# Two-layer diffusion trunk on one core: earlier modulation products and two weight loads outside the ring in layer 0

## The reference

```python
for l in range(2):
    sh, sc, g, shf, scf, gf = split6(silu(c) @ w_mod[l] + b_mod[l])     # modulation, per group
    h = rmsnorm(x) * (1 + sc) + sh
    if l == 0:
        q, k, v = split(h @ w_in_ab)            # 1024 x 2304; q and k normalised, sample rotated
        o = concat(grouped_query_attention, differential_attention) @ w_out_ab
    else:
        q, k, v = split(h @ w_in_c)             # 1024 x 3072
        o = attention(q, k, v) @ w_out_c
    x = x + g * o
    x = x + gf * moe(rmsnorm(x) * (1 + scf) + shf)   # 16 experts of 3 x 1024 x 1024, top 2
```

## Time and profile before

| what | value |
|---|---|
| median of three runs | 1276.59 us |
| span of the profiled execution | 1273.4 us |
| time of the profiled execution outside its span | not listed; the median is 3.2 us above the span |
| moved by DMA | 494.07 MB, 388 GB/s over the span |
| TensorE busy | 92% |
| VectorE, ScalarE, GpSimd busy | 22%, 15%, 4% |
| granted TensorE clock, mean | 0.978 |

### The profile page before, as it was taken

One profiled execution on the slowest core, in us unless ns is written; L12 is line 12 of the kernel. 1 busy time (PEld: TensorE's weight loads), 2 busy tenths in 40 slices (PEclk: granted clock), 3 DMA queues, 4 the chain that ended last, 5 costly groups with the idle time before them and its releaser, 6 DMA issues.

```text
span 1273.4 us, 13823 instructions
## 1 busy us (share of the span) xinstructions
PE 1174.6 (92%) x5485; PEld 514.1 (40%) x5485; DVE 283.2 (22%) x681; ACT 187.6 (15%) x441; POOL 56.4 (4%) x68
## 2 busy tenths in 40 slices
PE   4999999999888989899989999999998989888998
PEld 2445463343333434243334454643433434343333
DVE  1156441201020210101233443312020110102013
ACT  1234221100000101001022341210000101000010
POOL 0513000000000000000011100000000000000000
PEclk9999999999999999999999999899999999999999
DMA  9959999999999999999993679789999999999996
GB/s 376 340 207 353 419 419 427 428 415 431 426 429 429 428 428 429 429 428 428 416 393 85 262 263 424 305 366 421 376 428 428 428 429 428 429 429 429 428 429 256
DMA packets 58495, 494.07 MB, mean 388 GB/s; under 512 B 5314, under 2 KB 6482, under 8 KB 27732
## 3 DMA queue, kind: packets, MB, share of 16 engines
q1 hardware_dynamic: 55408, 485.85, 91.9%
q0 software_dynamic: 2864, 7.46, 1.8%
q10 hardware_dynamic: 180, 0.17, 0.0%
HBM read 490.69 MB, written 3.16 MB: 388 GB/s over the span
## 4 chain that ended last, share of the span: by engine, by line
PE 65%; DMA 25%; issue 3%; DVE 2%; POOL 2%; ACT 2%; SPq 1%; POOLq 0%; DVEq 0%
PE bank L1050 40%; DMA ring<-in_w_gate 10%; PE bank L825 9%; DMA ring<-in_w_up 9%; PE bank L835 3%; PE bank L1020 3%; PE bank L1011 3%; DMA ring<-in_w_in_ab 2%; PE bank L794 2%; DMA ring<-in_w_down 2%; PE bank L772 2%; DMA ring<-in_w_mod 1%; DMA gbuf<-gate_rows 1%; PE bank L1100 1%; POOL hss L672 1%
## 5 line engine op out<-in xcount | busy, mean ns | idle before, releaser
L1050 PE MATMUL bank<-ring,hT 128*64 128x512 f32 x2816 | 638.9, 609 | 63.8 <-issue 29.2
L1050 PEld LDWEIGHTS bank<-ring,hT 128*64 128x64 f32 x2816 | 213.9, 140 | 464.3 <-issue 462.5
L825 PE MATMUL bank<-ring,hT 128*128 128x512 f32 (+1 forms) x352 | 148.3, 580 | 3.9 <-DMA ring<-in_w_in_ab 2.4
L825 PEld LDWEIGHTS bank<-ring,hT 128*128 128x128 f32 x352 | 66.6, 192 | 79.6 <-issue 76.3
L1803 DVE TENSOR_TENSOR work<-work,bank 128x512 f32<-128x512 f32 x56 | 38.5, 688 | 188.6 <-PE bank L1020 188.4
L1796 DVE TENSOR_TENSOR work<-work,bank 128x512 f32<-128x512 f32 x32 | 22.0, 688 | 238.5 <-PE bank L1050 238.5
L1837 DVE COPY work<-bank 128x512 f32<-128x512 f32 x16 | 11.1, 691 | 228.9 <-PE bank L1050 212.4
L1011 PE MATMUL bank<-work 128*128 128x128 f32 x512 | 60.4, 277 | 0.0
L1011 PEld LDWEIGHTS bank<-work 128*128 128x128 f32 x512 | 59.3, 194 | 0.0
L835 PE MATMUL bank<-ring,work 128*128 128x512 f32 x128 | 56.5, 595 | 0.7 <-DVE work L1624 0.7
L1354 ACT ACTIVATE hT<-bank 128x512 f32<-128x512 f32 x32 | 19.0, 595 | 250.3 <-PE bank L1100 250.3
(11 more groups left out here) (211 smaller groups left out, 668.0 us busy)
## 6 DMA issues: line engine op xcount, KB each, us to landing
ring<-in_w_gate SPq DMA_DIRECT2D x64, 2048.0 KB, 17.2
ring<-in_w_up SPq DMA_DIRECT2D x56, 2048.0 KB, 17.2
ring<-in_w_down SPq DMA_DIRECT2D x56, 2048.0 KB, 16.9
ring<-in_w_mod SPq DMA_DIRECT2D x23, 2048.0 KB, 12.5
work<-in_w_up SPq DMA_DIRECT2D x8, 2048.0 KB, 20.9
ring<-in_w_in_c SPq DMA_DIRECT2D x6, 2048.0 KB, 21.1
ring<-in_w_in_ab SPq DMA_DIRECT2D x4, 2048.0 KB, 21.5
ring<-in_w_down SPq DMA_DIRECT2D x8, 1024.0 KB, 16.8
```

The source lines that it names most:

```text
L825: ins = pe.matmul(b[:, 0:n], hT[:, c, t * P:(t + 1) * P], w[:, c, 0:n], start=c == 0, stop=c == DC - 1)
L1050: ins = pe.matmul(bank[banks[j]][64 * e:64 * e + 64, :], lhs[:, 4 * h + c, 64 * e:64 * e + 64], weights(e, c, j), start=(h, c) == (0, 0), ...
```

## The change

The table `FILL` of layer 0 is written anew. Six modulation units of layer 0 are used between the projections of the prompt ahead of the first turn, and four of those that were used in turns 0 to 3 leave them. Input unit 4 of the prompt is used before its units 1, 2 and 3. Two units are loaded outside the ring: input unit 4 into `gbuf`, and modulation unit (0, 1, 2) into the buffers of the probabilities. ScalarE waits for the use of the latter before the first exponentials. `rot` moves to the buffer of the transposed q and k. The first two expert units of layer 0 are issued ahead of the up units outside the ring (`free = 2`, before 0). Layer 1's table is unchanged.

```diff
 FILL = {
     0: {"front": [("in", 0, 1), ("hT", 0, 0), ("in", 1, 1), ("in", 2, 1), ("in", 3, 1)],
-        "head": [("in", 4, 1), ("in", 0, 0), ("in", 1, 0)],
-        "keys": [("in", 2, 0)],
-        "scores": [("in", 3, 0)],
...
+        "head": [("in", 4, 1), ("mod", 0, 1, 0), ("in", 0, 0), ("mod", 0, 1, 1), ("in", 4, 0)],
+        "keys": [("mod", 0, 1, 2), ("mod", 0, 1, 3), ("in", 1, 0)],
+        "scores": [("mod", 0, 2, 0), ("in", 2, 0), ("mod", 0, 2, 1), ("in", 3, 0)],
...
+APART = {("in", 0, 4): "gbuf", ("mod", 0, 1, 2): "probs"}
+def ring_units(l):
+    return [u for u in dense_units(l) if u not in APART]
...
-        rot = work[:, 11264:13312]
+        rot = work[:, 8192:10240]
+        in_gbuf = gbuf[:, :, :].rearrange("p c n -> p (c n)").rearrange("p (c n) -> p c n", c=DC)
+        in_probs = work[:, 11264:15360].rearrange("p (r n) -> p r n", r=2)
...
-                free = 2 * l
+                free = 2
...
-            for g in range(N0):
+            for u in dense_units(0):
+                if u in APART:
+                    if u[0] == "in":
+                        sp.dma_start(in_gbuf, unit_src(u)).then_inc(gbuf_unit_loaded, 16)
+                    else:
+                        l, group, k = u[1:]
+                        sp.wait_ge(filled, fill(("hT", 0, 0, 0, 1)))
...
+                if (l, j) == (0, 0):
+                    act.wait_ge(mod_used, mods_used["mod", 0, 1, 2])
```

More of the change, by code:

```diff
@@ L107 @@
     0: {"front": [("in", 0, 1), ("hT", 0, 0), ("in", 1, 1), ("in", 2, 1), ("in", 3, 1)],
-        "head": [("in", 4, 1), ("in", 0, 0), ("in", 1, 0)],
-        "keys": [("in", 2, 0)],
-        "scores": [("in", 3, 0)],
[L111 to L115, removed]
+        "head": [("in", 4, 1), ("mod", 0, 1, 0), ("in", 0, 0), ("mod", 0, 1, 1), ("in", 4, 0)],
+        "keys": [("mod", 0, 1, 2), ("mod", 0, 1, 3), ("in", 1, 0)],
+        "scores": [("mod", 0, 2, 0), ("in", 2, 0), ("mod", 0, 2, 1), ("in", 3, 0)],
+        0: [("modT", 1), ("mod", 0, 2, 2)],
+        1: [("T", 0), ("mod", 0, 2, 3)],
+        2: [("mod", 1, 0, 0)],
+        3: [("oT", 1), ("mod", 1, 0, 1)],
+        4: [("wo", 0, 1)],
         5: [("wo", 1, 1)],
-        (6,): [("mod", 1, 0, 0)],
-        6: [("oT", 0)],
-        (7,): [("mod", 1, 0, 1)],
+        (6,): [("modT", 2)],
[1 row of a table added]
         7: [("hT", 1, 1), ("wo", 0, 0), ("rt", 1), ("wo", 1, 0), ("rc",), ("xT",), ("mod", 1, 0, 2),
@@ L368, in build @@
         ld_bias = sem("ld_bias")
+        gbuf_unit_loaded, probs_unit_loaded = sem("gbuf_unit_loaded"), sem("probs_unit_loaded")
         turns = sem("turns")
@@ L423, in build @@
                 k += 1
-        units = dense_units(0) + dense_units(1)
-        N0 = len(dense_units(0))
+        units = ring_units(0) + ring_units(1)
+        N0 = len(ring_units(0))
         mods_used = {u: i + 1 for i, u in enumerate(u for l in range(LAYERS) for u in released(l) if u[0] == "mod")}
         unit_no = {u: i for i, u in enumerate(units)}
-        free_order = [released(l) for l in range(LAYERS)]
+        free_order = [[u for u in released(l) if u not in APART] for l in range(LAYERS)]
         place, MOE_RING = {}, []
@@ L432, in build @@
             first = list(range(SLOTS)) if l == 0 else [MOE_RING[0][(i - OUTSIDE) % SLOTS] for i in range(SLOTS)]
-            mine = dense_units(l)
+            mine = ring_units(l)
             assert sorted(mine) == sorted(free_order[l])
@@ L628, in experts @@
                 return more
-            for g in range(N0):
+            for u in dense_units(0):
[5 more added lines that the diff above has]
+                        sp.wait_ge(filled, fill(("hT", 0, 0, 0, 1)))
+                        src = a["w_mod"][l].rearrange("(p r) n -> p r n", r=8)[:, 2 * k:2 * k + 2, GC * group:GC * (group + 1)]
+                        sp.dma_start(in_probs, src).then_inc(probs_unit_loaded, 16)
+                    continue
+                g = unit_no[u]
                 if g >= SLOTS:
@@ L777, in mod @@
                 halves = (l, group, k) == (0, 0, 3)
-                w = rows2[3 if halves else arrived(("mod", l, group, k))]
+                if ("mod", l, group, k) in APART:
+                    pe.wait_ge(probs_unit_loaded, 16)
+                    w = in_probs
+                else:
+                    w = rows2[3 if halves else arrived(("mod", l, group, k))]
                 if k == 0 and 3 * l + group:
@@ L818, in project @@
             def project(l, u, t):
-                w = ring[arrived(("in", l, u))]
                 n = unit_cols(("in", l, u))
+                if ("in", l, u) in APART:
+                    pe.wait_ge(gbuf_unit_loaded, 16)
+                    w = in_gbuf
+                else:
+                    w = ring[arrived(("in", l, u))]
                 b = bank_free(("qkv", l, u, t))
```

## The result

| kernel | median us | range | runs |
|---|---|---|---|
| before, beside the changed one | 1278.84 | 1272.77 to 1281.72 | 8 |
| changed | 1284.95 | 1284.05 to 1288.06 | 8 |

The ratio is 1.0053, with a 95% interval of 1.0040 to 1.0066: the change makes the kernel slower, by 6.1 us as the difference of the medians and by 6.8 us as the ratio has it. The profiled execution of the changed kernel took 1288.06 us, the slowest of its eight and 3.1 over its median, with a span of 1285.2 us and a mean granted clock of 0.974 (0.978 before). So the two profiles differ by more than the medians do; I compare places in them, not their ends.

A forecast was written before the change was run, and what follows sets the result against it. Layer 0's dense part was taken as TensorE-bound, its expert part as load-bound. From 1276.6, 5.1 us for later pair 2 units plus 1.0 for clock gave 1282.7 us; the range was 1274 to 1288.

The forecast's parts named there:

- The loads: Layer 0's dense part: loads land early, cost TensorE nothing; the 2.1 us wait at 205.04 goes, DMA engines idle there.
- Steps 1 and 2: Prompt's projections, then its q and k norm: projection about 14 us later, norm at 121.7; TensorE waits about 3.1 us.
- Step 3: Ahead of turn 4's scores: `modT` 1 lengthens VectorE's chain; TensorE waits 4.3 to 4.4 us, plus net 0.7 at turn 2's values.
- Step 4: Turns 3 to 5 of the attention: stay covered by one modulation product each and the output projections.
- Step 5: After the sample's second output projection: the chain takes 5.8 us against 2.8 of TensorE work; it waits 3.0 us.
- M: Start of the first expert product: forecast 198.7 us, from 188.5 plus 10.2 of added waits.
- From M to pair 2's last product: Expert part of layer 0: last units land at M + 141.8, from restart, 127.3 us of loads and 5.0 of slot waits.
- The sum: Pair 2's last units land at 340.5 against 335.4, 5.1 us later, and the shift stays; 1 us of clock added.
- the break-even: First expert product at 193.6 us, 5.1 us of added wait, where early loads and added waits cancel.
- That the early loads win: Rival: the chain stays covered, first expert product at 188.5, pair 2's last units at 330.3, kernel 1271.5 us; chance 0.12.
- That the two cancel: Rival: added TensorE waits and early loads balance, 1.4 to 8.9 us of wait, about 1277 to 1279 us; chance 0.22.
- That the loads collide with GpSimd's: Rival: GpSimd's small loads come late during the projections and delay the sample's transposes, some 1285 us; part of chance 0.66.

The follow-up runs named there:

- the order alone: Against the changed kernel: its order of work kept, but all units in the ring and the gate units where they were before; 1289.51 us, ratio 1.0084.
- the four early products: Against the changed kernel: only modulation group 1 used early, the other filler back in the turns; 1279.49 us, ratio 1.0004; run again 1279.7 us, ratio 1.0012.

## Why the prediction was right, by its steps

**The loads.** 60 to 120 us carries 371 to 387 GB/s ("well over 300"), no product waits for a load there, the up units come in time, and the hole near 204 is there. The fourth load of group 1 was to land at 75 us and landed at 79.0 (issued at 66.46, 12.5 us on its way), so it had 4.4 us to spare before its use and not 8. The cost of loads for TensorE was rightly taken at nothing in this order. It would not have been in the others: the order alone pays 3.6 us for late units, and four products in a row pay 4.19.

**Steps 1 and 2.** q and k were to come 14 us later; it was 15.05. A modulation product standing by itself takes 1.86 us from start to start (64.47 to 66.33 in the changed kernel), not the third of three in a row, 1.79, and the sample's transposes at 79.54 waited 0.57 us (0.31 before), which no step had. These two make about half of the 1.05 us. The waits of 1.0 and 2.1 us were 0.87 and 2.02.

**Step 3.** The wait of 4.3 to 4.4 us measures 4.0 at the full clock, and stands in two places. The kernel where `modT` 1 is moved shows its 1.5 us in the chain. The 0.7 us at the values of turn 2 were 0.54, 0.35 net.

**Step 4.** Turns 3 to 5 show no wait above 0.2 us.

**Step 5.** 3.0 us was over-sized: 2.14, in four waits and not one. The cause was named only in part. With `modT` 2 moved away from there the waits still add up to 2.22 us, so VectorE's work for it is not what opens them; what the run leaves is that nothing fills TensorE.

**M.** 198.7 was forecast and 201.04 measured. Of the 2.3 us between them 1.6 is the low clock inside the dense part, which the sum had booked elsewhere as 1 us. The granted clock was 0.50 in two stretches, behind the waits of 2.02 and 2.23 us. The Trainium skill, "TensorE: Matmul & The Clock Gate", section "Part 1: The HAM clock gate", has the clock follow how busy the engine has been; by that rule, which speaks against a change that thins the filler, the prediction would have put the full 1.7 us in place of 1. The trace agrees in the size, with 1.6. It doesn't show that such a wait always costs clock: the same wait of 2.01 us left it at 1.00 in the kernel with `modT` 2 moved.

**From M to pair 2's last product.** 141.8 was forecast; 143.0 was measured, and 142.9 to 143.3 in the eight other profiles in which modulation units were used early. The mis-sized term is the restart: the first two units issued at 208.2, behind the first product, landed at 215.9 and 221.8, so 13.6 us after their issue where the sum had 2.45 + 9.8 = 12.3.

**The sum.** Pair 2's last product was forecast 5.1 us later and stood 8.6 us later in these two profiles. That "the shift stays" from there on is not what these two profiles show: it was 11.9 us at layer 1's first expert product. The medians differ by 6.1 us, the very sum forecast, and by 5.1 to 8.4 within the interval. So the forecast was right in its sign, its mechanism and its size, but that it fits to 0.1 us is luck: M and the restart were 3.5 us short together, of which the 1 us for the clock makes good only a part, and the profiles' later growth has no place in it. The absolute time, 1282.7, lies 2.3 us under the result, as much as the median of before's eight runs lies over that of the three it started from (1278.84 against 1276.59). Two bounds were added up loosely: 12 us of wait and 1.7 of clock give 1285.2 and not 1286, and 3.8 us under the break-even is 1.3 us of wait and not 1.4.

**The rivals.** That the early loads win: the kernels with before's order and one unit outside show it in part, with M unchanged but for the start and 0 to 2.7 us gained; the bound of 5.1 us wasn't reached, since the slots were full at 97 us and the distance stayed at 144.5 to 146.1. That the two cancel: true of the four early products, at M = 192.77 and 195.96, whose ratios are 1.0004 and 1.0012; the break-even was put at 193.6. That the loads collide with GpSimd's: the sample's transposes waited 0.57 us against 0.31, no more.

## What to carry to other kernels

Work that fills an engine's waits is worth its length where it stands. Moved ahead of the producer that the waits hang on, it delays the producer by its own length and can leave the waits open, so that it is paid twice, as six modulation products did here. Before giving loads room to run ahead, ask what uses and frees the slots next: they can lead only by the slots, and a lead that ends in a full ring comes back as a hole. And price the two sides at the place where they meet (here pair 2's last units), not where each is seen best.

## What the runs showed of the hardware

- The clock fell behind waits as short as 2.02 and 2.23 us, and 8 and 10 dummy products of 0.24 us in their places kept it at 1.00. That took 1.6 us off the dense part, and nothing off the median of the kernel (1.0078 against 1.0053).
- The length of a wait alone doesn't tell whether the clock falls. The same expert product behind the same wait of 2.55 us took 7.09 us in the changed kernel (442.04) and 8.78 in the one with `modT` 2 moved (443.50).
- The start of the kernel differs with the clock from one execution to the next: the sample's fourth projection ended at 59.75 us in the profile with a mean granted clock of 1.00 from 20 to 40 us, at 61.09 where it was 0.79 from 20 to 28 us and 1.00 then, at 61.32 where it was 0.86 from 28 to 40 us, and at 64.09 where it was 0.80 and then 0.71. This is as large as most effects here, so that a profile has to be aligned at its start before its later times say anything.
